# Two feed-forward ends rearranged: accumulator banks, order of the last additions, and where the gate weights are split

## The reference, cut to what matters

```
f    = swiglu(rms_norm(h, ffn_pre_g[i]), w_ff_gate[i], w_ff_up[i], w_ff_down[i])    # 1024 -> 2816 -> 1024
h    = h + rms_norm(f, ffn_post_g[i])
gate = sigmoid(rms_norm(h, ple_norm_g[i]) @ w_ple_gate[i])                          # 1024 x 1024
h    = h + (p[i] @ w_ple_proj[i]) * gate                                            # 256 -> 1024
```

## Time and profile before

| | us |
|---|---|
| median of three runs | 1945.66 |
| lowest and highest | 1945.37, 1945.96 |
| span of the profiled execution, first to last instruction | 1944.6 |
| busy: PE, DVE, ACT, POOL | 1895.7, 1380.3, 895.7, 451.3 |
| granted TensorE clock, mean | 0.999 |

### The profile page before, as it was taken

One profiled execution on the slowest core, in us unless ns is written; L12 is line 12 of the kernel. 1 busy time (PEld: TensorE's weight loads), 2 busy tenths in 40 slices (PEclk: granted clock), 3 DMA queues, 4 the chain that ended last, 5 costly groups with the idle time before them and its releaser, 6 DMA issues.

```text
span 1944.6 us, 28061 instructions
## 1 busy us (share of the span) xinstructions
PE 1895.7 (97%) x9006; PEld 1553.0 (80%) x9006; DVE 1380.3 (71%) x2143; ACT 895.7 (46%) x1734; POOL 451.3 (23%) x480
## 2 busy tenths in 40 slices
PE   7799999999999999999999998999999999999998
PEld 7778888888888877888865787888888888888787
DVE  4987777777777787465579458777777777777863
ACT  6744443444444454343268446444444434443631
POOL 2311222222122221110036211221212222222210
PEclk9999999999999999999999999999999999999999
DMA  5333323233332351454330113323333232335201
GB/s 203 109 98 98 96 82 92 80 101 98 97 92 81 93 189 54 136 189 147 92 130 12 49 66 98 102 76 103 97 97 92 81 97 81 97 102 189 88 34 64
DMA packets 228486, 193.74 MB, mean 100 GB/s; under 512 B 13248, under 2 KB 205120, under 8 KB 228416
## 3 DMA queue, kind: packets, MB, share of 16 engines
q1 hardware_dynamic: 224144, 188.63, 30.6%
q10 hardware_dynamic: 4272, 4.21, 0.7%
HBM read 163.43 MB, written 16.78 MB: 93 GB/s over the span
## 4 chain that ended last, share of the span: by engine, by line
PE 88%; DVE 6%; ACT 2%; issue 2%; DMA 1%; POOL 1%; SPq 0%; DVEq 0%; ACTq 0%; POOLq 0%
PE ps L828 14%; PE ps L830 14%; PE ps L829 14%; PE ps L314 7%; PE ps L316 7%; PE ps L315 7%; PE ps L925 7%; PE ps L926 7%; PE ps L927 7%; PE ps L1667 1%; PE ps L1796 1%; PE ps L390 1%; PE ps L633 1%; DVE t_lo L1262 1%; PE ps L1746 1%
## 5 line engine op out<-in xcount | busy, mean ns | idle before, releaser
L1250 DVE TENSOR_TENSOR H<-H,ps 128x512 f32<-128x512 f32 x496 | 327.9, 685 | 112.8 <-PE ps L927 111.1
L1112 POOL TENSOR_TENSOR s_raw<-s_raw,a_raw 128x512 f32<-128x512 f32 x66 | 88.1, 1336 | 765.9 <-DVE s_lo L1163 648.8
L828 PE MATMUL ps<-t_hi,s_hi 128*128 128x512 f32 x528 | 206.3, 391 | 8.6 <-DVE t_lo L1262 5.6
L830 PE MATMUL ps<-t_hi,s_lo 128*128 128x512 f32 x528 | 205.5, 389 | 0.0
L829 PE MATMUL ps<-t_lo,s_hi 128*128 128x512 f32 x528 | 205.5, 389 | 0.0
L1001 ACT ACTIVATE m<-ps 128x512 f32<-128x512 f32 x44 | 26.4, 600 | 264.0 <-PE ps L830 261.6
L829 PE MATMUL ps<-b_lo,a_hi 128*128 128x512 f32 x352 | 137.0, 389 | 0.0
L828 PE MATMUL ps<-b_hi,a_hi 128*128 128x512 f32 x352 | 137.0, 389 | 0.0
L830 PE MATMUL ps<-b_hi,a_lo 128*128 128x512 f32 x352 | 136.9, 389 | 0.0
L925 PE MATMUL ps<-wd_hi,d_ab_hi 128*128 128x512 f32 x336 | 130.7, 389 | 0.0
L926 PE MATMUL ps<-wd_lo,d_ab_hi 128*128 128x512 f32 x336 | 130.7, 389 | 0.0
(11 more groups left out here) (296 smaller groups left out, 4891.7 us busy)
## 6 DMA issues: line engine op xcount, KB each, us to landing
a_raw<-in_w_ff_gate SPq DMA_DIRECT2D x88, 256.0 KB, 2.9
a_raw<-in_w_ff_up SPq DMA_DIRECT2D x88, 256.0 KB, 3.0
s_raw<-in_w_ff_up SPq DMA_DIRECT2D x88, 256.0 KB, 2.9
s_raw<-in_w_ff_gate SPq DMA_DIRECT2D x88, 256.0 KB, 3.1
wd_raw<-in_w_ff_down SPq DMA_DIRECT2D x44, 512.0 KB, 4.3
residual_spill<-H SPq DMA_DIRECT2D x24, 512.0 KB, 2.9
raw<-in_w_ple_gate SPq DMA_DIRECT2D x16, 512.0 KB, 5.4
back<-residual_spill SPq DMA_DIRECT2D x16, 512.0 KB, 5.0
```

Source lines behind the costliest of these rows:

```text
L828: pe.matmul(ps[:, bank, :], w[0], x[0], start=fresh and k == 0, stop=False, skip_group_check=not fresh)
L830: last = pe.matmul(ps[:, bank, :], w[1], x[0], start=False, stop=k == 3, skip_group_check=not fresh)
L1112: eng.tensor_tensor(form_raw(name), W_RAW[name][:, :, :], form_raw(other) if other != "A21" else W_RAW["A21"][:, :, :], op).then_inc(summe ...
L1250: dve.tensor_tensor(dst, dst, src, ALU.add).then_inc(F["summed"], 1)
```

## The change

Four things are done at the end of each feed-forward. In the diff below, comments at the end of a line name the function or the engine.

- The last half (`late`) writes S3 into banks 2 and 0 instead of 7 and 6, PE no longer waits for all adds of half 0 before S3 but before A11, and `d_adds` takes the last half's results in another order (`ADDS_LATE`). The gate product of even tiles goes to banks 4 and 5 and of odd tiles to 2 and 3 (the other way round before), so `kv_pe` gets a wait for the last tile's sigmoids.
- The hi parts of the gate weights are stored in another order of pieces (`GATE_HI_AT`). ACT makes hi parts 0 to 3 and DVE lo parts 0 and 1 inside the last tile of the feed-forward, hi parts 4 and 5 follow earlier than before, 6 and 7 when all down products are done. DVE makes lo parts 2 to 7 after its last adds. Each `gate_lo` waits for the one before it.
- The first gate product runs all hi-part matmuls of the eight k first, then the lo-part ones, with tile 1's `turn` ahead of k = 6. It starts when the adds up to A12 of row block 0 are done; the wait for all adds stands behind it. `keep_busy` goes, and tile 0's `turn` stands behind S4 of row block 0.
- ACT's order: squares of tiles 1 and 2 earlier, tile 0's and tile 1's gate-norm squares elsewhere, tile 1's behind the hi parts of `w_ple_proj`. POOL: the post-norm of tile 1 ahead of tile 0's gate norm.

```diff
+        ADDS_LATE = (("S3", 1, 1, 0), ("S3", 1, 1, 1), ("A12", 1, 0, 0), ("S1", 0, 1, 1), ("S1", 1, 1, 1), ("S4", 0, 0, 1),
+                     ("A12", 0, 0, 0), ("S3", 0, 1, 0), ("S3", 0, 1, 1), ("A22", 1, 1, 0), ("A22", 0, 1, 0), ("S4", 1, 0, 1))
+        LATE_BANKS = {("S3", 0): 2, ("S3", 1): 0}
...
         def ffn_pe_down(pe, L, g, h, beside, during=None):
...
                 if (name, j) == ("S3", 0):
                     pe.wait_ge(F["wd"], 4 * (GROUPS * L + g + 1))
-                    pe.wait_ge(F["summed"], SUMMED * (u + 1))
+                    if not late:
+                        pe.wait_ge(F["summed"], SUMMED * (u + 1))
                     pe.wait_ge(formed[0], formed[1] + 1)
                 if (name, j) == ("A11", 0):
+                    if late:
+                        pe.wait_ge(F["summed"], SUMMED * (u + 1))
                     pe.wait_ge(formed[0], formed[1] + 2)
...
             copy_u(act, L, g, t)                      # ffn_act_second
             if not is_last(g, t):
                 form_hi(act, "A11", L, *n)
+            else:
+                for k in range(2):
+                    gate_hi(act, L, k)
             gate_silu(act, L, g, t, 0)
             if not is_last(g, t):
                 form_hi(act, "S3", L, *n)
+            else:
+                for k in range(2, 4):
+                    gate_hi(act, L, k)
...
             if is_last(g, t):                         # ffn_dve_second
+                for k in range(2):
+                    gate_lo(dve, L, k)
                 up_first_half(dve, L, g, t)
...
+        GATE_HI_AT = (4, 5, 2, 3, 0, 1, 6, 7)
+        gate_w = [(Z["w_ple_gate_hi"][:, n, :], Z["w_ple_gate_lo"][:, k, :]) for k, n in enumerate(GATE_HI_AT)]
+        def gate_hi(act, L, k):
+            if k in (0, 2, 4):
+                act.wait_ge(F["product"], nth(("S3", "S2", "S1")[k // 2], L, *LAST_TILE))
+            if k == 6:
+                act.wait_ge(F["down"], PRODUCTS * (half_of(L, GROUPS, 0) + 1))
+            cut_hi(act, BASE[f"ple{L}"], k, gate_w[k][0])
+        def gate_lo(eng, L, k, columns=slice(0, D)):
+            base = BASE[f"ple{L}"]
+            if k in (0, 2, 4):
+                eng.wait_ge(F["product"], nth("S4" if k == 4 else "A12", L, *LAST_TILE))
+            if columns.start == 0:
+                eng.wait_ge(hi_done, base + k + 1)
+            if columns.stop == D:
+                eng.wait_ge(w_ready, base + k)
+            last = eng.tensor_tensor(gate_w[k][1][:, columns], raw[(base + k) % SLOTS][:, columns],
+                                     gate_w[k][0][:, columns].bitcast(F32), ALU.subtract)
+            if columns.stop == D:
+                last.then_inc(w_ready, 1)
+        def gate_bank(p, c):
+            return ps[:, 4 - 2 * p + c, :]
...
             if first_tile:                            # ple_pe
+                pe.wait_ge(F["summed"], added("A12", 0, half_of(L, GROUPS - 1, 1), True))
                 for k in range(KD):
+                    pe.wait_ge(hi_done, BASE[f"ple{L}"] + k + 1)
+                    for c in range(2):
+                        first_gate(pe, L, k, c, False)
+                for k in range(KD):
+                    if k == 6:
+                        turn(pe, s, 0, 1)
                     pe.wait_ge(w_ready, BASE[f"ple{L}"] + k + 1)
                     for c in range(2):
-                        last = gate(c, k)
+                        last = first_gate(pe, L, k, c, True)
...
-                    if k == KD // 2 - 1:
-                        turn(pe, s, 0, 1)
+                pe.wait_ge(F["summed"], SUMMED * (half_of(L, GROUPS, 0) + 1))
...
             pe.wait_ge(s["rotated"][p], s.free("rotated", i))      # kv_pe
+            if isinstance(i, int) and i == 0:
+                pe.wait_ge(G["sig"][p], done(TILES - 1))
...
                 ffn_post_rms(pool, L, 0)              # POOL
+                ffn_post_rms(pool, L, 1)
                 rms(f"ple{L}")(0, 0)
-                ffn_post_rms(pool, L, 1)
...
                 d_his(act, L, last, 0)                # ACT
+                gate_hi(act, L, 4)
                 gate_silu(act, L, last, 1, 1)
...
-                gate_cut(0)
+                gate_hi(act, L, 5)
                 ffn_post_act(act, L, 0)
                 for j in range(2):
                     d_copy_first(act, L, last, 1, j)
                 act.wait_ge(F["late_form"], 4 * (L + 1))
                 gain_row(f"ple{L}", I["ple_norm_g"][L])
+                ffn_post_act(act, L, 1)
+                d_copy_u(act, L, last, 1, 0)
                 tile_squares(0)
-                for j in range(2):
-                    d_copy_u(act, L, last, 1, j)
-                gate_cut(1)
-                ffn_post_act(act, L, 1)
-                gate_cut(2)
+                d_copy_u(act, L, last, 1, 1)
+                ffn_post_act(act, L, 2)
                 slot_hi(act, s_ple, 0, 0)
-                gate_cut(3)
-                ffn_post_act(act, L, 2)
-                gate_cut(4)
+                for k in range(6, KD):
+                    gate_hi(act, L, k)
                 act.wait_ge(F["ssum2"], TILES * L + 3)
-                tile_squares(1)
-                gate_cut(5)
-                act.wait_ge(F["down"], PRODUCTS * (half_of(L, GROUPS, 0) + 1))
-                for k in range(6, KD):
-                    gate_cut(k)
                 for k in range(2):
                     cut_hi(act, BASE[f"ple{L}"], KD + k, w_pp[0][:, k, :])
+                tile_squares(1)
                 p_hi(act, L, 0, 0)
...
                 def between(k):                       # DVE
-                    if k == 3:
-                        gate_cut(0)
-                    if k == 5:
+                    if ADDS_LATE[k][:2] == ("S1", 0):
                         dve.wait_ge(gain_loaded, 16 * GAIN[f"ple{L}"])
                         normed(dve, s_ple, 0, 0)
-                    if k == 8:
-                        gate_cut(1)
-                    if k == 9:
+                    if ADDS_LATE[k][:2] == ("A12", 0):
                         slot_lo(dve, s_ple, 0, 0)
...
                 d_adds(dve, L, last, 1, between=between)
-                gate_cut(2)
                 ffn_post(dve, L, 1)
-                gate_cut(3)
+                for k in range(2, 4):
+                    gate_lo(dve, L, k)
                 normed(dve, s_ple, 0, 1)
                 for k in range(4, KD):
-                    gate_cut(k)
+                    gate_lo(dve, L, k)
...
                 ffn_pe_down(pe, L, last, 1, (last, 1),             # PE
-                            lambda name, j: turn(pe, S[f"ple{L}"], 0, 0) if (name, j) == ("S1", 1) else None)
-                keep_busy(pe, 10, 2)
-                pe.wait_ge(F["summed"], SUMMED * (half_of(L, GROUPS, 0) + 1))
+                            lambda name, j: turn(pe, S[f"ple{L}"], 0, 0) if (name, j) == ("S4", 0) else None)
```

More of the change, by code:

```diff
@@ L783, in nth_add, with is_late, added, tile_added @@
             return SUMMED * (u + 1) + k + 1
+        def is_late(g, h):
+            return isinstance(g, int) and g == GROUPS - 1 and h == 1
+        def added(name, j, u, late):
+            return nth_add(max(k for k, x in enumerate(ADDS_LATE if late else ADDS) if x[:2] == (name, j)), u)
+        def tile_added(L, j):
+            h, u = j // 4, half_of(L, GROUPS - 1, j // 4)
+            return nth_add(max(k for k, x in enumerate(ADDS_LATE if h else ADDS) if 2 * x[2] + x[1] == j % 4), u)
         def ffn_load(sp, name, source, L, g, t):
@@ L918, in ffn_pe_down @@
                 if (name, j) == ("S4", 0):
-                    pe.wait_ge(F["summed"], nth_add(6, u))
+                    pe.wait_ge(F["summed"], added("S1", 0, u, late))
                 if (name, j) == ("S4", 1):
-                    pe.wait_ge(F["summed"], nth_add(8, u))
+                    pe.wait_ge(F["summed"], added("S1", 1, u, late))
                 fresh = name in ("A11", "S3")
@@ L940, in d_copy_first @@
             if j == 1:
-                act.wait_ge(F["summed"], nth_add(1, u))
+                act.wait_ge(F["summed"], SUMMED * (u + 1) if is_late(g, h) else added("S3", 0, u, False))
             act.activation(ps[:, (5, 7)[j], :], ps[:, (4, 3)[j], :], ACT.Copy).then_inc(F["d_copied"], 1)
@@ L947, in d_copy_u @@
             act.wait_ge(F["down"], nth_down("S2", j, u))
-            act.wait_ge(F["summed"], nth_add((3, 5)[j], u))
+            if j == 0:
+                act.wait_ge(F["summed"], SUMMED * (u + 1) if is_late(g, h) else added("S3", 1, u, False))
+            else:
+                act.wait_ge(F["summed"], added("A12", 1, u, is_late(g, h)))
             act.activation(ps[:, (6, 3)[j], :], ps[:, (5, 7)[j], :], ACT.Copy).then_inc(F["d_copied"], 1)
@@ L1239, in d_adds @@
         def d_adds(dve, L, g, h, first_group=False, between=None):
-            u, bank_of, begun = half_of(L, g, h), {x[:2]: x[2] for x in DOWN}, set()
-            for k, (name, j, q, c) in enumerate(ADDS):
```

(21 more changed lines are left out.)

12 lines of the change are left out of this document (5 added, 7 removed).

## The result

| us | before | after |
|---|---|---|
| median of five runs | 1945.66 | 1959.71 |
| lowest and highest | 1945.37, 1945.96 | 1958.83, 1961.6 |
| span of the profiled execution | 1944.6 | 1958.2 |
| its own time | | 1959.96 |
| granted TensorE clock, mean | 0.999 | 0.993 |

What follows compares the result with a forecast made beforehand. The prediction took DVE to set the time at each feed-forward's end, with PE following. Per layer 5.55 (4.95 + 0.6) plus 0.5 for the clock, 12.1 over both layers, gave 1957.8 us, range 1952 to 1963.

Steps and rivals of the forecast that it cites:

- The signs it named: Each layer: long PE and DVE waits, ACT waiting for a projection load, gate 3 to 4 us earlier, projection later, clock below 1.
- the two waits: Per layer, PE waits 7 to 8 us for a gate low cut; DVE about 6.6 before tile 1's `normed`.
- the shift of the projection: At each feed-forward's end, the projection starts 5 to 6 us later than in the kernel before.
- Early cuts, cost 0: Gate-weight cuts inside the last tile fit idle ACT and DVE time: cost 0, at most a few tenths per layer.
- First gate 3.8 earlier: After tile 0's chain, the first gate product starts at 723.55 instead of 727.37 in layer 0.
- Squares of tile 1 held by the second projection load: ACT's squares wait behind cuts needing that load (issued 731.53, landed 735.03), so tile 1's `normed` starts 4.95 us late.
- Linked waits, 0.6: Behind tile 1's `normed`, three of four DVE low parts wait on their predecessor, 0.19 each, 0.6 us per layer.
- Clock, 0.5 per layer: PE restarts at a slow clock after its long wait; bounds 0 and 2.4 us per layer, 0.5 taken.
- Sum: Projection delay 5.55 plus clock 0.5 gives 6.05 us per layer, +12.1 us for both layers.
- Not held by the loads: Rival: tile 1's squares aren't stopped and start at 729.04; 1.1 us per layer won, 1943.4 us; chance 0.09.
- PE was the bound: Rival: the earlier gate's 3.8 us are kept in both layers, giving 1938 us; chance 0.03.
- The clock stays low: Rival: projection and next gate run 4.8 us at half rate, costing 2.4 instead of 0.5, 1961.6 us; chance 0.17.

Runs made afterwards that it cites:

- experiment 1: Changed kernel with tile 1's squares moved ahead of the two high cuts of the projection weights on ScalarE; 1946.32 us, ratio 0.9999 to the kernel before.
- experiment 2: Kernel before the change, with only tile 1's squares moved behind the two high cuts of the projection weights; 1959.75 us, ratio 1.0071.
- experiment 5: Changed kernel with low parts 2 and 3 of the gate weights made early on GpSimd instead of VectorE; 1956.03 us, ratio 1.0059 to the kernel before.
- experiment 4: Changed kernel with 32 filler transposes on PE ahead of the low product of k = 4; 1961.32 us, ratio 1.0077 to the kernel before.

## Why the prediction was right

The mechanism was right at each step; one term was too small. The signs it named are all there, and the two waits and the shift of the projection are 1 to 3 us larger than named.

- *Early cuts, cost 0.* Right. The two hi parts ran from 689.98 to 691.98, the activation behind them started at 692.20, and DVE's two low parts filled its wait. The execution reached the adds of half 0 even 0.33 earlier.
- *First gate 3.8 earlier.* Right, 4.1. The turn was forecast at 720.12 and came at 719.79 aligned, without a wait.
- *Squares of tile 1 held by the second projection load.* Right as a mechanism (experiments 1 and 2), mis-sized: issue forecast at 731.53, came at 731.2 aligned; landing taken at 3.5 from the earlier trace rows, measured 5.3 and 6.1. In the kernel before the first load goes 3.6 us ahead; in the changed one both slots come free 1.3 us apart (1 MB of residual follows at once in both kernels). I took the landing of a load with the last one 3.6 us ahead for one that follows it by 1.3, though the step's own times for the two low parts, 730.18 and 731.50, put the loads that close. `normed` came 6.4 us later than before (739.51 aligned against 733.14) instead of 4.95.
- *Linked waits, 0.6.* Right: four low parts take 5.20 instead of 4.62.
- *Clock, 0.5 per layer.* The step was right, and the cost was 0, the lower bound: low products and turn run at half clock but faster than DVE feeds them, and PE waits 1.40 more just ahead of the projection. What is cited there from the Trainium skill on idle gaps is borne out for the clock, which fell to 0.50 in the wait of 9.38, and not for the time, because another engine set the pace. Experiments 1 and 5 show the price where PE sets it: 1.5 us and 2.3.
- *Sum.* Forecast 6.05 per layer. At the projections it is 7.0 (layer 0) and 7.6 (layer 1: 1836.02 to 1849.61 is 13.59, of which 6.00 stood already at that layer's adds, 1802.04 to 1808.04). Together 14.6; 0.33 was gained ahead and some 0.7 between the two ends, untraced: 13.6 of span. The median lies 1.5 above the profiled span, where the forecast took 1.1. So that 1957.8 came within 1.9 of 1959.71 is in part luck: the landings, 3.5 too small in all, stand against 1.0 for a clock that cost nothing and 1.0 gained outside the two ends.
- *Rivals.* "Not held by the loads" was given 1943.4; built, it ran at 1946.3, with the kernel before at 1946.22 beside it. DVE was the bound, as said, but two things were left out there: the half clock in layer 0, 1.5, and POOL's step held by DVE, with which `normed` came 1.25 and 1.54 (aligned) earlier than before instead of 1.7. "PE was the bound" falls with the same run. "The clock stays low" falls with the changed kernel's own windows (1.00 from 746 on, the projection at 748.29) and with experiment 4.

## What to carry to other kernels

On an engine that runs in order, ask of each instruction moved behind another what that other waits for; work that waits for a load whose slot a third engine frees belongs behind everything that is ready. A load's time is to be read from a place where the last load lies as far ahead of it in the queue. To hand VectorE's work to GpSimd, put it beside VectorE's reads of PSUM.

## What the runs showed of the hardware

- A GpSimd subtraction of 128x1024 (2.6 us) stops a VectorE operation on two SBUF tiles until it ends (0.42 became 2.44, 1.28 became 3.31) and doesn't touch VectorE's adds from PSUM (0.62). In the other direction, a GpSimd step on 128x1 beside VectorE's low part took 1.20 instead of 0.19.
- A 512 KB load took 3.5 us with the last one 3.6 us ahead of it and 1 MB right behind; 4.3 to 6.7 with the last one 1.3 us ahead and 1 MB behind; 4.2 and 4.7 with one 1.3 us ahead and nothing behind.
- The granted clock fell without a long standstill too: in kernel 1 PE ran at 0.50 from 742 to 744, though no wait of its end was longer than 1.92. What that takes, these runs don't tell.
